# Attention with context values in two places, loaded a head pair ahead, four probability buffers, and the loop over head pairs written out

## The reference, cut to what matters

```
s_loc = where(valid, q @ kg + bias, -inf)          # local window
s_ctx = q @ k_ctx                                  # cached context keys
p = softmax(concatenate([s_loc, s_ctx]))
o = p[..., :nk] @ vg + p[..., nk:] @ v_ctx
```

```
p = softmax(q @ k);  o = p @ v
```

## Time and profile before

| | |
|---|---|
| median of 3 runs | 3985.98 us (3980.12 to 3990.53) |
| profiled execution, its own time | 3985.86 us |
| its span (first to last instruction) | 3984.1 us |
| PE busy | 3646.8 us, 92% |
| DVE, ACT, POOL busy | 1535.5, 1035.3, 1229.5 us |
| attention stage, first scores to last `mix` | 2442.7 to 2855.4 us of the span |
| attention, `mix` of group 0 of pair 0 to that of pair 7 | 352.67 us for seven pairs |

### The profile page before, as it was taken

One profiled execution on the slowest core, in us unless ns is written; L12 is line 12 of the kernel. 1 busy time (PEld: TensorE's weight loads), 2 busy tenths in 40 slices (PEclk: granted clock), 3 DMA queues, 4 the chain that ended last, 5 costly groups with the idle time before them and its releaser, 6 DMA issues. The chain is left out here.

```text
span 3984.1 us, 49175 instructions
## 1 busy us (share of the span) xinstructions
PE 3646.8 (92%) x19244; PEld 3099.3 (78%) x19244; DVE 1535.5 (39%) x2498; ACT 1035.3 (26%) x1548; POOL 1229.5 (31%) x815
## 2 busy tenths in 40 slices
PE   8998788878999999999969996888899999999996
PEld 7786677666788888888858876888787888888885
DVE  2764443444533444434451113666432112211126
ACT  1431111123341111111152213666524111111113
POOL 1531111632532222222261212555334222222222
PEclk9998899989999999999979998999999999999998
DMA  2243222754121112111124336666301111111101
GB/s 112 93 156 101 85 95 74 227 179 176 68 74 64 69 63 80 70 69 64 64 97 165 142 130 170 158 158 158 122 27 37 38 38 38 38 38 38 41 34 58
DMA packets 175912, 369.18 MB, mean 93 GB/s; under 512 B 16983, under 2 KB 102487, under 8 KB 173560
## 3 DMA queue, kind: packets, MB, share of 16 engines
q1 hardware_dynamic: 170296, 356.21, 27.3%
q10 hardware_dynamic: 5440, 10.49, 0.8%
HBM read 286.93 MB, written 79.69 MB: 92 GB/s over the span
## 5 line engine op out<-in xcount | busy, mean ns | idle before, releaser
L145 POOL TENSOR_TENSOR w_lo<-w_raw,w_hi 128x1024 fp32r<-128x1024 f32 x214 | 512.4, 2394 | 1562.6 <-ACT w_hi L139 1562.6
L153 PE MATMUL ps_r<-a_hi,w_hi 128*128 128x512 f32 (+1 forms) x2112 | 541.0, 359 | 12.2 <-POOL a_lo L1378 9.8
L153 PE MATMUL ps_r<-a_lo,w_hi 128*128 128x512 f32 (+1 forms) x2112 | 536.7, 357 | 0.0
L153 PE MATMUL ps_r<-a_hi,w_lo 128*128 128x512 f32 (+1 forms) x2112 | 536.6, 357 | 0.0
L139 ACT ACTIVATE w_hi<-w_raw 128x1024 fp32r<-128x1024 f32 (+1 forms) x221 | 229.6, 1039 | 1169.5 <-PE ps_r L153 465.2
L153 PEld LDWEIGHTS ps_r<-a_hi,w_hi 128*128 128x128 f32 x2112 | 351.7, 188 | 83.5 <-POOL a_lo L1378 17.5
L153 PEld LDWEIGHTS ps_r<-a_lo,w_hi 128*128 128x128 f32 x2112 | 351.9, 188 | 62.6 <-issue 1.2
L153 PEld LDWEIGHTS ps_r<-a_hi,w_lo 128*128 128x128 f32 x2112 | 351.6, 188 | 62.7
L1555 DVE TENSOR_TENSOR hid_l<-hid_l,ps_r 128x1280 f32<-128x1280 f32 x44 | 65.6, 1490 | 848.9 <-PE ps_r L153 848.9
L1570 DVE SCALAR_TENSOR_TENSOR x_t_l<-ps_r,mod,x_t_l 128x1024 f32<-128x1024 f32 x320 | 268.1, 879 | 295.6 <-PE ps_r L153 295.6
L1405 POOL TENSOR_TENSOR hid_lo_l<-hid_l,hid_hi_l 128x1280 fp32r<-128x1280 f32 x44 | 140.4, 3191 | 517.7 <-ACT hid_hi_l L1324 517.7
(11 more groups left out here) (216 smaller groups left out, 6302.9 us busy)
## 6 DMA issues: line engine op xcount, KB each, us to landing
w_raw<-in_w_all SPq DMA_DIRECT2D x213, 512.0 KB, 3.2
ada_w_l<-in_ada_t SPq DMA_DIRECT2D x59, 512.0 KB, 3.2
q_hl<-q_d SPq DMA_DIRECT2D x64, 320.0 KB, 5.2
v_hl<-v_d SPq DMA_DIRECT2D x128, 128.0 KB, 2.7
t_tail_f<-in_ada_t SPq DMA_DIRECT2D x24, 512.0 KB, 3.8
k_hl<-k_d SPq DMA_DIRECT2D x32, 384.0 KB, 8.3
spec<-gout_f SPq DMA_DIRECT2D x80, 128.0 KB, 2.1
g_spec_c<-spec ACTq DMA_DIRECT2D x20, 512.0 KB, 4.6
```

The lines of the kernel that those rows point to most:

```text
L145: pool.tensor_tensor(wl[:, s, 0:width], raw[:, s, 0:width], wh[:, s, 0:width].bitcast(F32), ALU.subtract).then_inc(w_split, 1)
L153: last = pe.matmul(out[:, c0:c1], w[:, c % 2, blk * 128:blk * 128 + 128], x[:, c0:c1], start=start and b == 0 and term == 0, stop=stop and ...
```

## The change

- `vt` has 24 blocks in place of 20: the context values (cached and new) have two places, blocks 16 to 19 for even pairs and 20 to 23 for odd ones, with a semaphore each (`v_in[4]`, `v_in[5]` for the cached ones, `v_in[6]`, `v_in[7]` for the new ones).
- SP issues both loads of context values of pair i at the top of pass i, after the wait for all `mix` of pair i-2 (which used the place before). They were at its end, behind the wait for `mix` of group 8 (and 9) of pair i-1 and behind the load of queries and keys.
- Four probability buffers in place of three; unit u uses buffer u % 20 % 4, and DVE waits for the transposes of the unit four back, always.
- The bias tables `rpb_t` lie at `base_w`, over the weight buffer `w_raw`, which makes room: 8064 bytes of a partition are freed, and 6656 taken by the larger `vt` and `pb`.
- The two hardware loops (over pairs 0 to 6 on PE, ACT, DVE and POOL, over pairs 1 to 7 on SP) are written out.

```diff
             qq = sb("q_hl", [128, 2, 2, TOK], F32R, st)
             kk = sb("k_hl", [128, 2, 1536], F32R, st)
-            vt = sb("v_hl", [128, 20, 2, 128], F32R, st)
-            bias = sb("rpb_t", [128, 2, 16, RPB_W], F32, st)
+            vt = sb("v_hl", [128, 24, 2, 128], F32R, st)
+            bias = nc.alloc_sbuf_tensor_at("rpb_t", [128, 2, 16, RPB_W], F32, offset=base_w).ap()
             bm = sb("bias_m", [128, 2, 640], F32, st)
-            pb = sb("probs", [128, 3, 640], F32, st)
+            pb = sb("probs", [128, 4, 640], F32, st)
...
-            v_in = [sem(f"v_in{n}", st) for n in range(6)]
+            v_in = [sem(f"v_in{n}", st) for n in range(8)]
...
                 prologue()
                 step(0, 0, False)
-                with eng.Fori(0, 7) as i:
+                for i in range(7):
                     for g in range(1, G + 1):
                         step(i, g, False)
...
                     elif n == 4:
-                        sp.dma_start(vt[:, 16:18, :, :].bitcast(F32), vc_d[pair, :, :, :, :]).then_inc(v_in[n], 16)
+                        sp.dma_start(vt[:, 16 + 4 * (pair % 2):18 + 4 * (pair % 2), :, :].bitcast(F32), vc_d[pair, :, :, :, :]).then_inc(v_in[4 + pair % 2], 16)
                     else:
-                        sp.dma_start(vt[:, 18:20, :, :].rearrange("p b s d -> p b (s d)").bitcast(F32),
-                                     v_d[LS:TOK, pair, :, :].rearrange("(b k) s d -> k b (s d)", k=128)).then_inc(v_in[n], 16)
+                        sp.dma_start(vt[:, 18 + 4 * (pair % 2):20 + 4 * (pair % 2), :, :].rearrange("p b s d -> p b (s d)").bitcast(F32),
+                                     v_d[LS:TOK, pair, :, :].rearrange("(b k) s d -> k b (s d)", k=128)).then_inc(v_in[6 + pair % 2], 16)
...
-                with sp.Fori(1, 8) as i:
+                for i in range(1, 8):
+                    if i >= 2:
+                        sp.wait_ge(pv_mm, group_at(i, PV0 - G))
+                    load_v(i, 4)
+                    load_v(i, 5)
                     sp.wait_ge(s_mm, unit_at(i, 10 - U))
                     load_qk(i, 0)
...
                     sp.wait_ge(pv_mm, group_at(i, PV0 + 9 - G))
-                    load_v(i, 4)
                     load_v(i, 3)
                     load_bias(i, 1)
-                    sp.wait_ge(pv_mm, group_at(i, PV0 + 10 - G))
-                    load_v(i, 5)
...
                 def mix(i, g):
                     hh, j, _ = unit(2 * g)
                     if g == 0:
-                        pe.wait_ge(v_in[4], i * 16 + 16)
+                        pe.wait_ge(v_in[4 + i % 2], 16 * (i // 2) + 16)
                     if hh == 0:
                         if j is None:
-                            pe.wait_ge(v_in[5], i * 16 + 16)
+                            pe.wait_ge(v_in[6 + i % 2], 16 * (i // 2) + 16)
...
-                    v0 = 16 if j is not None else 18
+                    v0 = (16 if j is not None else 18) + 4 * (i % 2)
...
-                    before = u - (2 if u % U < 2 else 5 if u % U == 2 else 3)
+                    before = u - 4
                     if before >= 0:
                         dve.wait_ge(tc_mm, unit_at(i, before + 1))
```

More of the change, by code:

```diff
@@ L1999, in turn @@
                 def turn(dst, u, b):
-                    return pe.transpose(dst, pb[:, u % U % 3, 128 * b:128 * b + 128], ident[:, :])
+                    return pe.transpose(dst, pb[:, u % U % 4, 128 * b:128 * b + 128], ident[:, :])
                 def turn_local(i, u):
@@ L2065, in exps @@
                 def exps(i, u):
-                    p, q = pb[:, u % U % 3, 0:width(u)], stat[:, u % 4, :]
+                    p, q = pb[:, u % U % 4, 0:width(u)], stat[:, u % 4, :]
                     act.wait_ge(sm_ok, unit_at(i, u + 1))
@@ L2129, in norm @@
                 def norm(i, u):
-                    p = pb[:, u % U % 3, 0:width(u)]
+                    p = pb[:, u % U % 4, 0:width(u)]
                     pool.wait_ge(rr_ok, unit_at(i, u + 1))
@@ L2164, in minima @@
                     dve.sem_inc(turn_v, 1)
-                    dve.tensor_tensor_reduce(out=pb[:, u % U % 3, 0:w], in0=ps_s[u % 2][:, 0:w], in1=bm[:, u % 2, 0:w],
+                    dve.tensor_tensor_reduce(out=pb[:, u % U % 4, 0:w], in0=ps_s[u % 2][:, 0:w], in1=bm[:, u % 2, 0:w],
                                              scale=1.0, scalar=3.0e38, op0=ALU.add, op1=ALU.min,
```

## The result

| | before | after |
|---|---|---|
| median of 4 runs | 3987.1 us (3980.12 to 3990.53) | 3946.07 us (3942.36 to 3951.2) |
| ratio, 95% interval | | 0.99, 0.9882 to 0.9918 |
| profiled execution, its own time | 3985.86 us | 3942.36 us |
| `mix` of group 0 of pair 0 to that of pair 7 | 352.67 us | 316.19 us |

The account below looks back on a forecast made before the run. PE's waits in the attention stage set the pace, no other engine being the bound. Terms 17.5 + 6.6 + 6.7 + 1.0 - 1.1 + 0.8 = 31.5 us off 3985.98 gave 3954 us, range 3945 to 3973 (8 in 10).

Parts of the forecast that it names:

- transfer, steps to group 0: PE's waits ahead of `mix` of group 0 in pairs 1 to 7 go with the earlier load: 17.5 us.
- clock, steps to group 1: Clock falls in the step after `mix` of group 0 vanish: five at 1.32 us, 6.6 us; at worst none.
- fourth buffer, steps to group 8: Unit 20's `minima` on DVE no longer waits for unit 18's transposes: 0.95 us in seven pairs, 6.7 us.
- other minima: Second `minima` of other steps on DVE also wait less with four buffers: 1.0 us, between 0 and 10.9.
- given back: Two steps after `mix` of group 0: other engines' catch-up during PE's wait is lost, returning as waits: -1.1 us.
- form: Writing out the attention stage's loops, judged from pair 7 against pair 4: 0.8 us gained, between 0 and 1.6.
- late next: Ahead of `mix` of group 0, nothing else was to be late once the load came early.
- the label `pt_lo` is true: Rival: in pairs 4 to 6 PE really waits for `pt_lo`, 6.4 us, two clock falls stay; 3963.5 us, 5%.
- the waits go, the clock still falls: Rival in attention: remaining PE waits suffice for the fall, or part of 17.5 returns; 3961 us, to 3972; 17%.
- The range: For 8 in 10: 3945 to 3973 us, the upper end with half the first term and the clock given back.
- Code arriving late: Rival: PE's code late at block boundaries in attention; 17 blocks, none hidden, cost 46 us, giving 4000 us; slower 9%.

Follow-up runs that it names:

- reorder: Kernel before, with only the cached context values loaded ahead of the second head's queries and keys on SP: median 3963.25 us, ratio 0.994.
- loops_vals: Changed kernel with three probability buffers and the old buffer wait again; loops written out, context values in two places: median 3967.19 us, ratio 0.9952.
- loops: Kernel before, with only its two hardware loops written out; values in one place, three buffers: median 3986.18 us, ratio 1.0003.
- bufs: Kernel before, with four probability buffers and the bias tables at their new place; hardware loops kept: median 3991.15 us, ratio 1.0004.
- looped2: Changed kernel with PE, ACT, DVE and POOL looping again, three passes of two pairs; SP and pairs 6, 7 written out: median 3966.44 us, ratio 0.995.

## Why the prediction was right, and where its sizes were off

The term by term comparison for the seven pairs, from the steps of both traces (sums over the seven steps of a kind):

| step of the forecast | forecast, us | measured, us |
|---|---|---|
| transfer, steps to group 0 | 17.5 | 50.99 - 32.94 = 18.1 |
| clock, steps to group 1 | 6.6 | 39.76 - 31.80 = 8.0, of which five falls 7.1 |
| fourth buffer, steps to group 8 | 6.7 | 38.80 - 32.55 = 6.3 |
| all else (other minima 1.0, given back -1.1, form 0.8) | 0.7 | 4.2 |
| sum | 31.5 | 36.5 |

The five falls are counted against 4.67 us, the same step in pair 4, where the clock stayed up; the forecast had counted them against 4.73, the step to group 6.

- **The load.** Right in place, size and cause: reorder takes the wait away with nothing but an earlier issue. What was forecast to be late next (nothing) held. The rival that the label `pt_lo` is true fell: no wait is left in pairs 4 to 6.
- **The clock.** It stays up, as forecast, but the forecast's reason was too simple, and this term came out right in part by luck. I took the fall to hang on the late load alone. loops_vals has no late load and the clock falls all the same, behind the shorter wait ahead of group 8. So in the written-out kernel the values and the buffers were both needed for the 6.6 us, and the buffers were there for another reason. In the loop the early load was nearly enough (reorder: one fall). Why the same wait costs the clock in loops_vals and not in loops is open. The rival "the waits go, the clock still falls" named a true danger.
- **The fourth buffer.** Right with the load gone: 0.95 us per pair was forecast, 1.02 is what it gives in the written-out kernel (5.67 to 4.65, loops_vals) and 0.80 in the loop (bufs). The other minima, taken at 1.0, are worth some 1.5 by the steps to groups 0 to 7 of loops_vals. That the buffer is worth nothing while the load is late (bufs) the forecast did not say: it added up parts that stand in series ahead of one and the same transfer.
- **The loops written out.** This is the term that was mis-sized: 0.8, with a bound of 1.6. looped2 against pair 6 gives 0.07 to 0.10 us for each step, 5 to 7 us for the 70 steps (less in loops, 0.05 us each, where the late load and three buffers stayed). The forecast compared seven steps of pair 7 with seven of pair 4 as one sum, 0.16 us. The single steps were there to be read: six of them were together 0.48 us shorter in pair 7 (five shorter, one 0.03 longer), and the one to group 2 was 0.32 longer (4.53 against 4.21); its reason was not looked for (the same 0.34 us wait for POOL's `probs` stands in it in both pairs). The bound of 1.6 rested on that sum and was no bound.
- **What is given back** was not separable from this.
- **The range.** One sum of the prediction is off. With the clock and half of the first term lost, 31.5 - 6.6 - 8.75 = 16.2 us are left, which is 3970 us, and not 14 and 3972. The upper end of the range, 3973, has the same slip. It does not bear on the outcome.
- **Code arriving late**, the slower rival: 18 more blocks were fetched, as worked out, and no wait of PE of the forecast's 2.7 us goes with them. In the seven pairs, the one step of the changed kernel that is clearly longer than its like in other pairs in both profiles is that to group 4 in pair 3, 4.86 in place of 4.53 us; its cause was not measured. What looks like the rival's mechanism shows in looped2, but at a taken branch, not in written-out code. The Trainium skill, page "Runtime: NRT & Kernel Launch", section "Instruction fetch mechanics", has it so: fetching in sequence is mostly hidden, and a taken branch to code out of reach waits for a fetch. The trace of looped2 is in keeping with it, with 8.01 us at DVE's branch; in the kernel before, whose loop body is one pair, the step behind the branch shows no such stall (4.67 us in pair 4).

The predicted time, 3954, lies 8 us above the measured 3946.07, inside its range: 5.0 us of it from the stretch, most of them the form of the code. The other 3 us are within the spread of the runs (3942.36 to 3951.2).

## What to carry to other kernels

When several parts of a change save time ahead of one late transfer, they do not add up: price them in the order of the chain, and look first for what ends it. Here one load moved in the queue gave 24 of the 41 us, and the two other edits gave nothing until it was done. When two stretches of the same work are compared, compare step by step before summing, since one odd step can hide a steady difference.

## What was not expected of the hardware

- A hardware loop whose body was two pairs stalled DVE for 8.01 and 7.97 us at its branch, with code fetched on the instruction queue q14 meanwhile; loops of one pair showed no such stall. That the fetch is the cause is argued, not shown.
- Steps written out, with constants in the place of registers in their waits, ran 0.07 to 0.10 us shorter in looped2 (steps of 4.1 to 4.7 us), on an engine that showed no idle time for it. Which instructions make it up was not measured.
- The granted clock fell behind a wait of 1.5 us in loops_vals, in six pairs of seven (0.83 over 10 us, 0.50 from 2600 to 2602), while PE was busy 8.9 of those 10 us. Behind a wait of 1.4 us in reorder it fell once in seven pairs, behind the same wait of 1.5 us in loops never.
- The feed-forward part took 840.0 us in 13 of the 14 profiled executions, and 835.2 in the other.
